# Six blocks of projections instead of eight, and the next phase's entry work inside the last two

## What is computed

```python
h = rmsnorm(x, g_norm1) * (1 + sc1) + sh1
proj = h @ w_in                        # 1024 -> hg 1024, mb 1288, rw 896 columns
o_hg = hgrn2_chunked(q, k, v, logf)    # S_t = diag(f_t) S + k v^T, gated by silu(hg_g)
xbc = silu(conv4(mb_xbc))              # x, B and C of mamba
y_mb = (ssd_chunked(x, dt, A, B, C) + D * x) * silu(mb_z)
o_rw = rwkv7_scan(r, logw, k, v, kk, a)
x = x + g1 * (concat(o_hg, y_mb, o_rw) @ w_out)
x = x + g2 * ((silu(h2 @ w_gate) * (h2 @ w_up)) @ w_down)
```

## Time and profile before

| | us |
|---|---|
| three runs | 1986.57, 1989.53 (median), 1996.15 |
| profiled execution | 1990.94, of which the span in the trace 1989.2 |
| PE matmul busy | 1666.2 (84%) |
| DVE busy | 977.0 (49%) |
| ACT busy | 589.8 (30%) |
| POOL busy | 253.4 (13%) |

### The profile page before, as it was taken

The page is one execution under the profiler, slowest core; times in us unless marked ns, Lnnn a source line. Parts: engine busy times, 40 slices in busy tenths (PEclk is TensorE's granted clock), DMA queues, the critical chain, the costliest instruction groups (busy, mean ns, idle before and its releaser), DMA issues.

```text
span 1989.2 us, 31929 instructions
## 1 busy us (share of the span) xinstructions
PE 1666.2 (84%) x13471; PEld 1509.8 (76%) x13471; DVE 977.0 (49%) x2105; ACT 589.8 (30%) x1055; POOL 253.4 (13%) x331
## 2 busy tenths in 40 slices
PE   4898888887888537578888887999969999999995
PEld 2898777776877423246677777988869999999995
DVE  5405436665643256756666734545653333433335
ACT  2324223312322132123433434333342212222222
POOL 3501001110100022103233341000000000000000
PEclk9899889888988757668888989999989999999998
DMA  8110001010100045432121232433312131221311
GB/s 298 38 53 22 22 17 38 29 40 26 58 30 29 11 159 170 146 97 58 55 62 54 70 116 86 122 106 104 124 54 82 56 97 56 74 86 55 98 47 54
DMA packets 199013, 149.22 MB, mean 75 GB/s; under 512 B 6447, under 2 KB 187168, under 8 KB 197592
## 3 DMA queue, kind: packets, MB, share of 16 engines
q1 hardware_dynamic: 188482, 120.67, 20.1%
q0 software_dynamic: 7440, 23.27, 3.4%
q10 hardware_dynamic: 2950, 3.24, 0.5%
HBM read 134.03 MB, written 13.18 MB: 74 GB/s over the span
## 4 chain that ended last, share of the span: by engine, by line
PE 68%; DVE 18%; ACT 6%; DMA 4%; issue 3%; POOL 0%; SPq 0%; POOLq 0%; DVEq 0%; ACTq 0%
PE bank L1240 17%; PE bank L1241 17%; PE bank L1242 17%; PE bank L1179 3%; DMA RAW<-in_w_ada 1%; PE bank L1592 1%; PE bank L1591 1%; ACT WHI L1764 1%; PE bank L1427 1%; PE bank L1428 1%; PE bank L1376 1%; PE bank L1383 1%; PE bank L1438 1%; PE bank L1385 1%; PE bank L1248 1%
## 5 line engine op out<-in xcount | busy, mean ns | idle before, releaser
L1240 PE MATMUL bank<-HBH,WHI 128*128 128x328 f32 (+1 forms) x832 | 261.7, 315 | 14.8 <-DVE HBL L2319 10.1
L2202 DVE TENSOR_TENSOR WLO<-RAW,WHI 128x1024 fp32r<-128x1024 f32 (+4 forms) x149 | 152.3, 1025 | 237.5 <-ACT WHI L1764 236.9
L1764 ACT CAST WHI<-RAW 128x1024 fp32r<-128x1024 f32 (+4 forms) x210 | 187.9, 898 | 250.8 <-PE bank L1242 244.5
L1241 PE MATMUL bank<-HBL,WHI 128*128 128x328 f32 (+1 forms) x832 | 260.2, 313 | 0.0
L1242 PE MATMUL bank<-HBH,WLO 128*128 128x328 f32 (+1 forms) x832 | 259.4, 312 | 0.0
L1240 PE MATMUL bank<-HHI,WHI 128*128 128x344 f32 x624 | 212.8, 341 | 11.8 <-DVE HLO L2415 5.9
L1241 PE MATMUL bank<-HLO,WHI 128*128 128x344 f32 x624 | 205.3, 329 | 0.0
L1242 PE MATMUL bank<-HHI,WLO 128*128 128x344 f32 x624 | 204.7, 328 | 0.0
L1003 POOL TENSOR_TENSOR WLO<-RAW,WHI 128x1024 fp32r<-128x1024 f32 (+1 forms) x61 | 130.5, 2143 | 502.5 <-ACT WHI L1764 502.5
L1240 PEld LDWEIGHTS bank<-HBH,WHI 128*128 128x128 f32 x832 | 157.7, 190 | 16.4 <-issue 16.2
L1242 PEld LDWEIGHTS bank<-HBH,WLO 128*128 128x128 f32 x832 | 157.9, 190 | 0.0
(11 more groups left out here) (554 smaller groups left out, 3152.6 us busy)
## 6 DMA issues: line engine op xcount, KB each, us to landing
RAW<-in_w_gate SPq DMA_DIRECT2D x44, 512.0 KB, 3.9
RAW<-in_w_up SPq DMA_DIRECT2D x44, 512.0 KB, 3.9
RAW<-in_w_ada SPq DMA_DIRECT2D x32, 512.0 KB, 4.6
RAW<-in_w_in SPq DMA_DIRECT2D x26, 512.0 KB, 3.8
ADAW<-in_w_ada SPq DMA_DIRECT2D x8, 1024.0 KB, 19.9
RAW<-in_w_out SPq DMA_DIRECT2D x16, 512.0 KB, 4.2
RAW<-in_w_down SPq DMA_DIRECT2D x32, 256.0 KB, 2.7
RAW<-in_w_down SPq DMA_DIRECT2D x16, 384.0 KB, 3.5
```

Of the source, the lines that this page charges most:

```text
L1240: mm(bank[:, 0:w], whi[:, k, :], hi_k, start=(k == 0), stop=False)
L1241: mm(bank[:, 0:w], whi[:, k, :], lo_k, start=False, stop=False)
L1764: a.copy(w_split(i)[0][:, 0:nk, :], RAW[u % NRAW][:, 0:nk, :]).then_inc(w_hi, 1)
L2202: v.tensor_tensor(wlo[:, 0:nk, :], RAW[u % NRAW][:, 0:nk, :], whi[:, 0:nk, :].bitcast(F32), ALU.subtract).then_inc(w_lo, 1)
```

## The change

The full stop between the phases goes. `end_phase(..., 1)` is removed on all four engines; what it protected is now guarded by single waits. To free HHI and HLO early, the 54 projections are packed closer: `BEHIND` also names lora and seq0, so there are nine a block, and the last is placed behind gates in block 5. The silu items begin in block 0. Blocks 6 and 7 have no projections. A table `ENTRY` places there what `pre` did, in pieces, and hg blocks 0 and 1 as well, with the logits of hg block 2. `rw_final` is cut into five `fin` pieces, of which the last (the rw state) is the first item of `PLAN2`. In the loops of phase 2 hg runs two blocks ahead of mamba (`HGA = 2`), so loops 6 and 7 have no hg work, and loop 5 prepares none. `FILL` still acts at the places of the missing items, which gives loop 7 two more matmul groups. To make this fit, `XB` moves to the place of HHI and HLO, and the mb work tensors move to where `XB` was.

```diff
@@ -771,8 +770,9 @@
                 rw_list.append(('rw_' + n, b))
                 if front and b + 1 < NB:
                     rw_list.append(('rw_' + front, b + 1))
-        BEHIND = {'turn': 1, 'lin': 1, 'gates': 1, 'inv4': 1, 'post': 1, 'decay': 2}
+        BEHIND = {'turn': 1, 'lin': 1, 'lora': 1, 'gates': 1, 'inv4': 1, 'seq0': 1, 'post': 1, 'decay': 2}
         silu = list(range(3 * 6))
+        brought = [0]
 
         def fill1(n):
             for _ in range(n):
...
+
+        ENTRY = {
+            ('rw_turn', 6): [('entry', 0)],
+            ('rw_lora', 7): [('xs', 0), ('xs', 1), ('xs', 2)],
+            ('rw_inv3', 6): [('xs', 3), ('xs', 4), ('xs', 5)],
+            ('rw_inv4', 6): [('hg_logits', 0)],
+            ('rw_inv5', 6): [('hg_gate', 0)],
+            ('rw_fold', 6): [('hg_levels', 0)],
+            ('rw_seq0', 6): [('hg_att', 0)],
+            ('rw_seq1', 6): [('hg_state', 0)],
+            ('rw_post', 6): [('hg_o', 0), ('hg_logits', 1)],
+            ('rw_turn', 7): [('hg_sq', 0), ('hg_gate', 1)],
+            ('rw_inv1', 7): [('fin', 0), ('pre', 0)],
+            ('rw_inv2', 7): [('hg_out', 0), ('hg_levels', 1)],
+            ('rw_inv3', 7): [('pre', 1), ('fin', 1)],
+            ('rw_inv4', 7): [('hg_att', 1)],
+            ('rw_inv5', 7): [('hg_state', 1), ('pre', 2)],
+            ('rw_fold', 7): [('hg_o', 1), ('fin', 2)],
+            ('rw_seq0', 7): [('hg_sq', 1), ('pre', 3)],
+            ('rw_seq1', 7): [('hg_logits', 2), ('fin', 3)],
+            ('rw_post', 7): [('hg_out', 1)]}
         for item in rw_list:
             PLAN1.append(item)
             if item == ('rw_gates', NB - 1):
                 PLAN1.append(('rws0', 0))
             fill1(BEHIND.get(item[0][3:], 0))
-            if item[0] in ('rw_lin', 'rw_inv2', 'rw_lora', 'rw_inv3') and silu and (
-                    item[1] >= (4 if item[0] in ('rw_lin', 'rw_lora') else 3)):
+            if item[0] in ('rw_lin', 'rw_inv2', 'rw_lora', 'rw_inv3') and silu and silu[0] + 1 < brought[0]:
                 PLAN1.append(('silu', silu.pop(0)))
-        assert not silu
-        fill1(len(left))
-        PLAN1.append(('ev', QP1 - 1))
-        PLAN1.append(('rw_final', 0))
-
-        PLAN2 = [('pre', 0), ('hg_logits', 0), ('mb_turn', 0), ('hg_gate', 0), ('hg_levels', 0)]
+            if ('entry', 0) in ENTRY.get(item, []):
+                assert not left
+            PLAN1 += ENTRY.get(item, [])
+        assert not silu and not left
+
+        PLAN2 = [('fin', 4), ('mb_turn', 0), ('hg_gate', 2), ('hg_levels', 2)]
         late = list(range(QP1, QP2))
         samples = list(SAMPLES)
         FILL = {'hg_att': 2, 'mb_decay': 2, 'hg_o': 2, 'mb_prod': 2, 'mb_turn': 2, 'hg_levels': 2}
         for b in range(NB):
-            items = [('hg_att', b), ('hg_state', b), ('mb_decay', b), ('hg_o', b), ('hg_logits', b + 1), ('mb_prod', b),
-                     ('hg_sq', b), ('hg_gate', b + 1), ('mb_turn', b + 1), ('mb_sq', b), ('hg_out', b),
-                     ('hg_levels', b + 1), ('mb_out', b), ('hg_x', b)]
+            h = b + HGA
+            items = [('hg_att', h), ('hg_state', h), ('mb_decay', b), ('hg_o', h), ('hg_logits', h + 1), ('mb_prod', b),
+                     ('hg_sq', h), ('hg_gate', h + 1), ('mb_turn', b + 1), ('mb_sq', b), ('hg_out', h),
+                     ('hg_levels', h + 1), ('mb_out', b), ('hg_x', b)]
             for item in items:
-                if item[1] == NB or (item[0] == 'hg_x' and b > 2):
+                if item[0] == 'hg_x' and b > 2:
                     continue
-                PLAN2.append(item)
+                if item[1] < NB:
+                    PLAN2.append(item)
                 if samples and item[0] != 'mb_out':
                     PLAN2.append((samples.pop(0), 0))
```

The entry as POOL runs it, the loop over PLAN1 that reaches it, and the new waits of PE's att item:

```diff
+            def entry():
+
+                pool.wait_ge(dense_done, QP1)
+                pool.wait_ge(acc_out, 16 * 18)
+                for k in range(2):
+                    pool.wait_ge(stg_out[k], 16 * 9)
+                load_hg(0)
+                for t in range(6):
+                    pool.dma_start(XB[t][:, :], xbd[t]).then_inc(mb_loaded[t], 16)
+                load_hg(1)
+                pool.dma_start(DTB[:, :], mb_dt_bias.broadcast_to([P, 8])).then_inc(pre_dma, 16)
+                pool.dma_start(AEX[:, :], mb_A_log.broadcast_to([P, 8])).then_inc(pre_dma, 16)
+                link(g.memset(HSH[:, :, :, :], 0.0))
+                link(g.memset(HAD[:, :, :], 0.0))
+                g.memset(HVD[:, :, :, :], 0.0).then_inc(pre_pool, 1)
...
+                elif what == 'entry':
+                    entry()
+                elif what == 'hg_att' and arg + 2 < NB:
+                    load_hg(arg + 2)
+                elif what == 'fin' and arg == 3:
+                    shift_conv_out()
...
                     pe.wait_ge(hgf_dve, step(HGF_DVE, 'factors', b))
-                    if b:
-                        pe.wait_ge(mb_act, step(MB_ACT, 'rs', b - 1))
-                    if 0 < b <= 3:
-                        pe.wait_ge(x_act, 9 + b)
-                        pe.wait_ge(x_dve, 9 + b)
+                    if b == 0:
+                        pe.wait_ge(evac['act'], EVN[QP1 - 1])
+                    else:
+                        pe.wait_ge(hg_act, step(HG_ACT, 'rs', b - 1))
+                    if b > HGA:
+                        pe.wait_ge(mb_act, step(MB_ACT, 'rs', b - HGA - 1))
+                    if 0 < b - HGA <= 3:
+                        pe.wait_ge(x_act, 9 + b - HGA)
+                        pe.wait_ge(x_dve, 9 + b - HGA)
```

The pieces of `pre` on ACT, and of the last copies on DVE:

```diff
+            def silu_xb(t):
+
+                tables(GATES_SET)
+                act.wait_ge(mb_loaded[t], 16)
+                if t >= 2:
+                    act.wait_ge(silu_m, 18 + t - 1)
+                a.activation(PSG[t % 2][:, :], XB[t][:, :], ACT.Sigmoid).then_inc(silu_s, 1)
...
+            def pre(k):
+
                 tables(LN_EXP)
...
+                if k == 0:
+                    act.wait_ge(pre_dma, 32)
+                    a.activation(AEX[:, :], AEX[:, :], ACT.Exp).then_inc(pre_act, 1)
+                    act.wait_ge(pre_dve, PRE_DVE.index('nabs') + 1)
+                    link(a.activation(DTE[:, :, :], DTN[:, :, :], ACT.Exp))
+                    a.activation(DTE[:, :, :], DTE[:, :, :], ACT.Ln, bias=1.0).then_inc(pre_act, 1)
+                elif k == 1:
+                    act.wait_ge(pre_dve, PRE_DVE.index('dta') + 1)
+                    a.activation(DTE[:, :, :], DTA[:, :, :], ACT.Exp).then_inc(pre_act, 1)
+                elif k == 2:
+                    act.wait_ge(pre_dve, PRE_DVE.index('es') + 1)
+                    a.activation(ES[:, :, :], ES[:, :, :], ACT.Exp)
...
+            def fin(k):
+
+                dve.wait_ge(fin_pe, k + 1)
+                dst, src = ((FSH[:, 0:512], BK8[3][0:9, :]), (FSH[:, 512:896], BK8[3][0:9, 0:384]),
+                            (FCV[:, 0:512], BK8[3][0:11, :]), (FCV[:, 512:768], BK8[3][0:11, 0:256]),
+                            (FST[:, :, :].rearrange("v j k -> v (j k)"), BK8[3][0:64, 0:256]))[k]
+                v.tensor_copy(dst, src).then_inc(fin_dve, 1)
```

342 lines of the change are left out of this document (165 added, 177 removed).

## The result

The changed kernel takes 2018.1 us (median of 4 runs, 2015.45 to 2024.64), the kernel before 1992.45 us beside it (1986.57 to 1996.15). The ratio is 1.0136, 95% interval 1.011 to 1.0163. The forecast was 1989 us and a range up to 2018, so the time lies just above it, on its slow side. The profiled execution took 2018.21 us with a span of 2016.4, against a span of 1989.2 before: 27.2 us more.

What follows compares the result with a forecast made beforehand. PE was taken as nearly full in rw blocks and loops, with 44.32 us of full stop where it is busy 6.5; 23 + 8 - 33 = -2 on 1990.9 us gave 1989 us, range 1965 to 2018.

Steps and rivals of the forecast that it cites:

- Term 1: Blocks 0 to 5: 12 projections come earlier and 4 go away; +23 us (12 to 42).
- Behind seq0: Added projection after the first state step, five blocks: fills a 0.70 us wait, may restore full clock; 0.5 each, 2.5 us.
- The projection behind LoRA and the convolutions: Added projection at full length, 3.75 us a block; 18 convolutions sharing one ACC buffer, packed closer, +5 us.
- rival S2: Blocks 1 to 3: convolutions wait for each other's store, seq0 projections cost 4.3 each; likelier +12, 2001 us; 0.14 with N.
- Term 2: Blocks 6 and 7 and the stop: work removed against two hg blocks and entry work added; +8 us (-10 to +28).
- I take 14.4 (4.8 at its end as above, 9.6 for the other four): Path time saved by removing block 6's seven projections, 14.4 us (10 to 20): three at its end, four elsewhere.
- 40 for hg, 4.4, 2.6, 5 and 5, less 31: Blocks 6, 7: two hg blocks, XB products, two table loads, rest of entry, half-clock small matmuls; less the stop's saving.
- rival S1: Blocks 6 and 7 fall to half clock without projections, decided by a clock under about 0.65; +20, 2009 us; chance 0.18.
- Rival N: The stop only moves: POOL's entry waits for block 6's last hg stores, XB lands late; a few us; 0.14 with S2.
- Term 3: Loops 5 to 7 of phase 2, from which hg work is gone; -33 us (-24 to -37).
- That leaves 38 us if PE never waits, and I take 38: Loop 6: without hg's PE work and half clock, and with no waits, it takes 38 us, -17.8.
- PE is what is late next: Loops 5 to 7: once hg is gone, PE is the engine that sets the time; no size given.

Runs made afterwards that it cites:

- pack: The kernel before with only the closer packing: nine projections a block, none in blocks 6 and 7, full stop and loops kept; 2023.9 us, ratio 1.015.
- hg_behind: The changed kernel with all hg stages of blocks 0 and 1 moved from rw blocks 6 and 7 to behind the last one; 2027.37 us, ratio 1.0171.
- pack_inv2: The kernel before, packed to nine projections, with the ninth behind inverse step 2 instead of behind seq0; 2036.66 us, ratio 1.0227.

## Why the prediction was wrong, step by step

**Term 1.** The step that failed is "Behind seq0 ... I take 0.5 each, 2.5 us". It measured 15.0 us in five blocks, 3.0 each in the mean, with the moved convolutions in it. A plain block shows the same shortfall without them: both added projections together were 3.75 + 0.5 = 4.25 us in the sum and cost 7.0 (blocks 1 and 4) to 8.3 (block 0). I let the clock pay for it: the projection would bring back full clock for the second state step and for the three projections behind the norm. It did so for the state step, which in block 1 takes 2.6 us from its first matmul on ST to its last instead of 4.2. It did not for the three projections. In the kernel before, block 1 runs them from 291.12 to the turn at 303.84, 12.7 us; in the changed kernel, with one more ahead, from 307.77 to the turn at 320.99, 13.2 us:

```profile
283.01 0.47 PE L1427 MATMUL bank<-AR,ST 64*64 64x64 f32 x2 [0.69 <-DVE UV L2619]
...
286.74 0.42 PE L1430 MATMUL bank<-UV,BKt 128*64 128x64 f32 x2
...
291.12 0.85 PE L1240 MATMUL bank<-HHI,WHI 128*128 128x344 f32 x1
...
303.84 0.60 PE L1179 MATMUL bank<-ident,AR 128*128 128x128 f32 x4
```

```profile
301.21 0.32 PE L1458 MATMUL bank<-AR,ST 64*64 64x64 f32 x2 [0.69 <-DVE UV L2673]
...
303.52 0.28 PE L1461 MATMUL bank<-UV,BKt 128*64 128x64 f32 x2
...
307.11 1.22 PE L1469 MATMUL bank<-OSQ,headsum 128*128 128x256 f32 x2 [1.05 <-DVE OSQ L2565]
307.77 0.85 PE L1271 MATMUL bank<-HHI,WHI 128*128 128x344 f32 x1
...
320.99 0.60 PE L1208 MATMUL bank<-ident,AR 128*128 128x128 f32 x4
```

The head sums between them wait for DVE twice (1.05 us before the second), and the first projection matmul behind takes 0.85 us in both kernels. The clock that the ninth projection bought was gone again there. Without that hope the price is 3.75 - 0.7 = 3.05, and the row for it, the wait of 0.70 in the earlier trace rows, was in my hands. That this equals the mean of 3.0 is partly luck, as the mean is made of 4.6, 1.9, 6.4, 0.1 and 1.9. The projection behind LoRA and the convolutions were right together, 18.75 + 5 forecast for blocks 0 to 4 and 23.2 measured, and that is luck too: the first cost up to 5.1 in plain blocks instead of 3.75, the convolutions less than 5. Of rival S2 the mark in blocks 2 and 3 came (78.2 and 78.5 us), but block 4 gave its own 7.6 us back, since the convolutions had left it. Over blocks 2 to 4 they cost 12.6 us above three plain blocks of 72, against 10.8 before. Some 3.0 us of block 2 are the silu items, which the change also moved: pack, which leaves them where they were, takes 75.2 us there.

**Term 2, what is removed.** The step that failed is "I take 14.4 (4.8 at its end as above, 9.6 for the other four)". With 3.5 for block 7 it was 17.9 us in all, of which the table load of 1.28 stands in the packed kernel too. Of the other 16.6 the packed kernel shows 5.5 (5.2 in block 6, 0.3 in block 7 with the stop). The three at the end of the block were worth what I took, 4.8. The other four were worth almost nothing. They had covered waits for DVE and ACT beside the next block's front work, of 4.64 us and of 1.97 where 0.47 stands with them (another of 1.61 stands in both kernels), and kept the small matmuls near full clock. I had read block 7 as proof that six projections and the front work cost 20.1 us together, and gave the projections more than half of it. The front work has nearly all of it: with it and without projections the block is 63.3 us long, without both 44.6.

**Term 2, what is added.** 26 us net of the stop were forecast (40 for hg, 4.4, 2.6, 5 and 5, less 31), and the changed kernel stands 174.56 - 152.15 = 22.4 us above the packed one in the same stretch. The total was right, and that hg hides in almost nothing was shown by hg_behind. But hg took some 46 us instead of 40, so the small terms beside it must have taken less than I gave them; that the two cancel is luck. The function tables were right too: five loads in block 6 instead of three. The clock was in the sum with 5 us, under rival S1 with 20 more. Rival N did not come: in blocks 6 and 7 no engine's wait ends on a load of XB.

**Rival S1** had the right mechanism and a chance of 0.18. Its mark was a clock under 0.65, and it came to 0.58 and 0.56. Its price on the path is not measured, but its size in PE's time is: 12.1 us in block 6 from the removal of the projections alone, and 8.3 us in block 7 between pack's clock of 0.73 and pack_inv2's 0.50, where the block was 7.9 us longer. In the changed kernel added matmuls brought back 9.3 us of PE's time in block 6 at 0.74. The row that I gave for S1, loop 2 with its many small matmuls, was not the reason: the packed kernel falls to 0.61 in block 6 with no hg matmul in it. The Trainium skill ("TensorE: Matmul & The Clock Gate", Loop structure matters more than you think), which I had named beside S1, says that the loop nest decides whether matmuls stay at full clock, and its bad case is a long wait for a transfer ahead of every matmul. The rows agree in direction, with shorter waits and for DVE and ACT: with the projections between the waits block 6 ran at 0.88, without them at 0.61.

**Term 3.** Forecast -33, measured -22.7. The step that failed is "That leaves 38 us if PE never waits, and I take 38" for loop 6. From one sum on T to the next it takes 46.8 us instead of 55.7, -8.9 where I had -17.8:

```profile
1056.92:1112.64 55.72, 47.64 (x459) 41.73 (x459) 37.29 (x92) 18.80 (x33) 18.31 (x13) 0.91 0.25 72
```

```profile
1107.15:1153.98 46.83, 39.09 (x213) 34.42 (x214) 17.12 (x38) 12.81 (x20) 17.75 (x13) 0.93 0.29 85
```

(the kernel before and the changed one). The 246 small matmuls of hg are gone and PE is busy for 8.6 us less, near the forecast's 7 and 3. But PE still idles for 7.7 us, where it idled for 8.1. In the shorter loop the groups that multiply by `w_out` wait for DVE: 3.3 us until it has added an earlier result to XTA, which frees the bank, and 1.9 us for their input MIXR. The view of groups names it:

```profile
L1271 PE MATMUL bank<-MIXR,WHI 128*128 128x384 f32 x32 | 12.4, 386 | 5.2 <-DVE XTA L2329 3.3 <-DVE MIXR L2384 1.9
```

"PE is what is late next" was said without a check, and DVE was late next. Loop 5, measured in the same way, gave 1.3 us instead of 3.3. Loop 7 with the part behind it gave 14.1, somewhat more than the forecast's 11.4: 10.3 us of PE's work moved from behind the loops into loop 7, which became 0.6 us shorter all the same.

**Together** the three misses are +15, +9 and +10 us, all on one side, and loops 0 to 4 took 5 off. Each of the first two came from giving a projection's 3.75 us a value other than the one its neighbours set: too little where PE was nearly full, too much where waits and small matmuls stood around it. I read the two errors as one of kind, which is why they did not cancel and the range was too narrow.

## What to carry to other kernels

Filler work on TensorE between the steps of a dependent chain has two prices, and moving it changed both in this kernel: where it went, PE was nearly full and it cost about its length; where it left, its waits opened up and the small matmuls around it slowed down, so that of 26 us only 5 came back. Before packing, take PE's busy time in both places and ask for the removed piece what it covered. To end a full stop, move into the last block only the work for which its waits have room: the entry's 9 us on DVE cost 0.3 us there, while of two hg blocks, a chain of their own of some 51 us, only 5.4 were hidden.
